# Rwkv scan on one core: second BETA times V and first inverse in turn ahead of level 2, keys of both chunks in turn

## The reference, cut to what matters

```python
def wkv7_scan(s0, r, w, kk, a, k, v):
    def step(s, inp):
        r_t, w_t, kk_t, a_t, k_t, v_t = inp
        s_kk = jnp.einsum('bhvk,bhk->bhv', s, kk_t)
        s = (s * w_t[:, :, None, :] - s_kk[..., None] * (kk_t * a_t)[:, :, None, :]
             + v_t[..., None] * k_t[:, :, None, :])
        return s, jnp.einsum('bhvk,bhk->bhv', s, r_t)
```

## Time and profile before

| | |
|---|---|
| median of 3 runs | 3761.28 us (3754.23 to 3763.72) |
| profiled execution | 3748.89 us |
| its span | 3747.1 us |
| mean granted TensorE clock | 0.904 of full |
| TensorE matmul busy | 3128.4 us (83%) |
| VectorE busy | 1132.6 us (30%) |
| the scan in the trace | from about 447 to 992 us |

### The profile page before, as it was taken

One profiled execution on the slowest core, in us unless ns is written; L12 is line 12 of the kernel. 1 busy time (PEld: TensorE's weight loads), 2 busy tenths in 40 slices (PEclk: granted clock), 3 DMA queues, 4 the chain that ended last, 5 costly groups with the idle time before them and its releaser, 6 DMA issues. The chain is left out here.

```text
span 3747.1 us, 61863 instructions
## 1 busy us (share of the span) xinstructions
PE 3128.4 (83%) x27303; PEld 2140.8 (57%) x27303; DVE 1132.6 (30%) x1902; ACT 544.8 (15%) x995; POOL 198.7 (5%) x170
## 2 busy tenths in 40 slices
PE   3998489999887999985999999875977488877874
PEld 1454378888533444442999999862436254544442
DVE  0302477777442111345111111014013562110112
ACT  0001233333201000011000010101011141100001
POOL 0000012111100000000100000000001000100000
PEclk8999689999979999987999999987985698899997
DMA  8322312211405324604677777723100104899995
GB/s 348 125 70 78 93 50 56 69 51 27 152 3 124 97 79 153 250 35 153 200 271 279 245 256 279 251 76 113 68 1 0 62 1 180 335 427 426 427 427 201
DMA packets 246708, 612.13 MB, mean 163 GB/s; under 512 B 27188, under 2 KB 136278, under 8 KB 230968
## 3 DMA queue, kind: packets, MB, share of 16 engines
q1 hardware_dynamic: 217704, 522.93, 37.9%
q10 hardware_dynamic: 15968, 54.41, 3.8%
q0 software_dynamic: 12784, 30.99, 3.0%
HBM read 565.64 MB, written 42.63 MB: 162 GB/s over the span
## 5 line engine op out<-in xcount | busy, mean ns | idle before, releaser
L2655 PE MATMUL ps<-moe_xt,moe_wb 128*128 128x152 f32 (+1 forms) x3520 | 457.2, 292 | 2.5 <-DVE moe_xt L2817 1.9
L2655 PEld LDWEIGHTS ps<-moe_xt,moe_wb 128*128 128x128 f32 x3520 | 452.5, 194 | 3.1 <-issue 3.1
L1614 PE MATMUL ps<-ffn_h,ffn_wb 128*128 128x512 f32 x704 | 304.2, 595 | 15.5 <-PEq L1509 15.5
L2333 PE MATMUL ps<-hier_wb,hier_xt 128*64 128x256 f32 x2048 | 241.1, 391 | 73.7 <-DMA hier_wb<-in_expert_w_up 38.1
L2333 PEld LDWEIGHTS ps<-hier_wb,hier_xt 128*64 128x64 f32 x2048 | 160.0, 141 | 166.2 <-issue 66.2
L1614 PEld LDWEIGHTS ps<-ffn_h,ffn_wb 128*128 128x128 f32 x704 | 134.4, 191 | 185.3 <-issue 185.3
L2662 PE MATMUL ps<-moe_hT,moe_wb 128*128 128x152 f32 (+1 forms) x1760 | 227.2, 290 | 0.0
L2662 PEld LDWEIGHTS ps<-moe_hT,moe_wb 128*128 128x128 f32 x1760 | 222.7, 190 | 0.0
L834 PE MATMUL ps<-AT,X 64*64 64x64 f32 x4608 | 162.5, 225 | 33.2 <-DVE X L1120 18.1
L834 PEld LDWEIGHTS ps<-AT,X 64*64 64x64 f32 x4608 | 152.1, 139 | 44.9 <-issue 24.3
L1683 PE MATMUL ps<-ffn_g,ffn_wd 128*128 128x512 f32 x352 | 153.0, 598 | 2.6 <-PEq L1577 2.6
(11 more groups left out here) (487 smaller groups left out, 4063.8 us busy)
## 6 DMA issues: line engine op xcount, KB each, us to landing
moe_wb<-in_moe_w SPq DMA_DIRECT2D x60, 2048.0 KB, 10.4
hier_wb<-in_expert_w_gate SPq DMA_DIRECT2D x32, 2048.0 KB, 38.1
hier_wb<-in_expert_w_up SPq DMA_DIRECT2D x32, 2048.0 KB, 38.1
hier_wb<-in_expert_w_down SPq DMA_DIRECT2D x32, 2048.0 KB, 38.4
moe_wb<-in_moe_w SPq DMA_DIRECT2D x30, 1536.0 KB, 7.7
wb_ada<-in_ada_w SPq DMA_DIRECT2D x8, 3072.0 KB, 18.5
ada_late<-in_ada_w ACTq DMA_DIRECT2D x8, 3072.0 KB, 9.6
ffn_wb<-in_ffn_w SPq DMA_DIRECT2D x22, 1024.0 KB, 7.8
```

The lines of the kernel that those rows point to most:

```text
L1614: mm = pe.matmul(k.ps[:, bank + q, :], wb[:, j, q, c, o * P:(o + 1) * P], h[:, c, :], start=c == 0, stop=c == KC - 1)
L2333: mm = pe.matmul(k.ps[both_halves(a), bank, 0:256], xs[:, c, :], wb[:, slot, at:at + 256], start=c == 0, stop=c == KC - 1)
L2655: mm = pe.matmul(k.ps[:, bank, 0:width], wb[:, slot, at:at + P], xs[:, c, :], start=c == 0, stop=c == KC - 1)
```

## The change

In `b_times_v` and `inverse_times` the single products become functions (`one_b_times_v`, `one_inverse_times`) with the same operands and places in PSUM. The first chunk's BT times V and the second chunk's inverse keep their places. The first chunk's inverse leaves its place behind level 2: it is issued ahead of level 2, right behind `prep_sums`, where the second chunk's BT times V already stood, and product by product in turn with that. Both now stand behind the waits of both. The keys of both chunks are issued head by head in turn. The number of products is unchanged.

```diff
+                def inverse_and_second_b_times_v(n):
+                    need(pe, w_taken, 2 * n + 1)
+                    need(pe, updated, 2 * NL * (n + 1))
+                    need(pe, bt_sb, min(n + 2, TILES))
+                    need(pe, gt_sb, outputs(min(n + 1, TILES - 1)))
+                    for h in range(2 * HP):
+                        b = one_b_times_v(n, 1, h)
+                        t_w = one_inverse_times(n, 0, h)
+                        if h == 2 * HP - 1:
+                            b.then_inc(bv_ps, 1)
+                    t_w.then_inc(u_ps, 1)
...
-                def keys_to_state(n, step):
-                    if step == steps(n):
-                        return
-                    r = rows_of(chunk_of(n, step))
+                def keys_to_state(n):
...
                     for h in range(2 * HP):
-                        cols = slice(h * C, (h + 1) * C)
-                        pe.matmul(k.ps[half(h), 4 + step, hcols(h)], tok_k[r, n % 2, cols], V[r, n % 3, cols],
-                                  start=h < 2, stop=False)
+                        for step in range(steps(n)):
+                            r, cols = rows_of(chunk_of(n, step)), slice(h * C, (h + 1) * C)
+                            pe.matmul(k.ps[half(h), 4 + step, hcols(h)], tok_k[r, n % 2, cols], V[r, n % 3, cols],
+                                      start=h < 2, stop=False)
...
                     if nxt:
                         prep_sums(n + 1)
                     if prev:
-                        b_times_v(n - 1, 1)
+                        inverse_and_second_b_times_v(n - 1)
                     if now:
                         level_change(n, 2)
                     if prev:
-                        inverse_times(n - 1, 0)
-                        keys_to_state(n - 1, 0)
-                        keys_to_state(n - 1, 1)
+                        keys_to_state(n - 1)
                         betas_to_state(n - 1, 0)
```

More of the change, by code:

```diff
@@ L865, in prep_sums, with one_b_times_v @@
                     mm.then_inc(sums_ps, 1)
[L867 to L876, removed]
+                def one_b_times_v(n, step, h):
+                    r = rows_of(chunk_of(n, step))
+                    return pe.matmul(k.ps[r, 2 + h % 2, hcols(h)], BT[r, n % 2, slot(h), :],
+                                     V[r, n % 3, h * C:(h + 1) * C], start=h < 2, stop=False)
@@ new lines, in one_inverse_times, with first_b_times_v @@
+                def one_inverse_times(n, step, h):
+                    r = rows_of(chunk_of(n, step))
+                    return pe.matmul(k.ps[r, 2 + h // 8, h % 8 * C:h % 8 * C + C], TT[r, slot(h), :],
+                                     wb[r, h * C:(h + 1) * C], start=True, stop=True)
+                def first_b_times_v(n):
+                    need(pe, bt_sb, n + 1)
+                    need(pe, v_landed[n % 3], 16 * (n // 3 + 1))
+                    need(pe, u_taken, 2 * n)
+                    need(pe, gt_sb, outputs(n))
@@ L877, in b_times_v @@
                     for h in range(2 * HP):
-                        mm = pe.matmul(k.ps[r, 2 + h % 2, hcols(h)], BT[r, n % 2, slot(h), :],
-                                       V[r, n % 3, h * C:(h + 1) * C], start=h < 2, stop=False)
+                        mm = one_b_times_v(n, 0, h)
                     mm.then_inc(bv_ps, 1)
+                def inverse_and_second_b_times_v(n):
[9 more added lines that the diff above has]
+                    t_w.then_inc(u_ps, 1)
@@ L882, in kappa_times_state, with second_inverse_times @@
+                def second_inverse_times(n):
+                    need(pe, w_taken, 2 * n + 2)
+                    for h in range(2 * HP):
+                        mm = one_inverse_times(n, 1, h)
+                    mm.then_inc(u_ps, 1)
                 def kappa_times_state(n, step):
@@ L890, in kappa_times_state @@
                     mm.then_inc(w_ps, 1)
-                def inverse_times(n, step):
-                    r = rows_of(chunk_of(n, step))
[L894 to L902, removed]
-                def keys_to_state(n, step):
-                    if step == steps(n):
-                        return
-                    r = rows_of(chunk_of(n, step))
+                def keys_to_state(n):
                     if n + 2 < TILES:
@@ L999, in _ @@
                             output_from_state(n - 1)
-                        inverse_times(n - 1, 1)
+                        second_inverse_times(n - 1)
                     if now:
@@ L1005, in _ @@
                     if now:
-                        b_times_v(n, 0)
+                        first_b_times_v(n)
                         last_turn(n)
```

## The result

The changed kernel takes 3733.81 us in the median of 5 runs (3727.72 to 3738.91), against 3754.23 us for the kernel before on the same chip (3749.52 to 3763.72). The ratio is 0.9941 with a 95% interval of 0.9920 to 0.9961: 22 us faster, at the least 15. The forecast was 9 us faster, and the range ended at 3740. The wait that the forecast counted is gone, but the gain is twice its size.

What follows compares the result with a forecast made beforehand. A tile was a VectorE stretch, then a TensorE stretch, joined by the wait at L1161. Gains of 3.1, 4.4, 1.1 and 0.5 us summed to 9.1, from the median 3761.28 to 3752.2 us; range 3740 to 3766.

Steps and rivals of the forecast that it cites:

- The wait that the forecast counted: VectorE's wait at L1161 for the betas of step 0, ahead of the new state: 0.68 us in iteration 8, 13.4 in all.
- The pair takes 1.93 us in place of 3.55: First inverse and b_times_v in turn ahead of level 2 run at a level's pace, saving TensorE 1.62 us a tile.
- The rival that the two would not run in turn: Shared PSUM banks hold the pair to 3.6 us, level 2 comes late, ten tiles lose 0.6 us each: 3767; chance 0.05.
- The keys at the pace of four quarters: Keys of both chunks in turn take output_from_tile's 1.07 us in place of 1.69, saving 0.62.
- They are worth nothing beside the pair: Even without any gain on the keys, the betas' sum comes 0.9 us before VectorE needs it.
- u is taken behind the exponentials, VectorE's wait goes, TensorE waits some 1.3 us for level 3's masks: At the joint: u there 2.6 us earlier, VectorE's 0.68 us wait gone, a new TensorE wait ahead of level 3.
- 9.1 us from the wait: Over the scan: 3.1 us from context iterations, 4.4 from latent ones, 1.1 from iteration 11, 0.5 from the last.
- The last iteration: 0.5 us: The pair waits until 973.15 for TT's update and ends at 975.1 in place of 975.7.
- What is lost at the tile's end: Rival: TensorE's stop in level 5, up to 4.32 us, swallows the latent 4.4 us (3756.6) or all (3761); chance 0.15.
- the clock falls; this is the case on the other side: Rival: the new wait ahead of level 3 lowers the clock, 1.8 us each, 20 us in eleven iterations: 3772; chance 0.1.
- TensorE's saving arrives whole: Rival: VectorE's stretch is not the limit, so TensorE's saved work counts in full, some 26 us: 3735; chance 0.1.

Runs made afterwards that it cites:

- the pair alone: Against the kernel before, only the first inverse and b_times_v in turn ahead of level 2, keys one chunk after the other as before: 3734.53 us, ratio 0.9948.
- small loads: Both kernels, with r, k and kk loaded on 8 of 128 partitions from the second tile on: 3805.30 us (kernel before) and 3795.65 us (changed).
- late loads: Both kernels, with hw and ha loaded first and r, k and kk held until BT is kept: 3734.72 us (kernel before) and 3714.52 us (changed).
- the keys alone: Kernel before with only the keys of both chunks in turn, everything else as before: 3750.15 us, ratio 0.9986.
- the inverse moved but not paired: As the changed kernel, keys in turn included, but b_times_v first and then the first inverse, not in turn: 3753.73 us, ratio 0.9997 to the kernel before.
- the betas late: Changed kernel with the betas of step 0 issued behind level 3 in place of ahead of it: 3786.29 us, ratio 1.0087.

## Why the prediction was wrong

Point by point:

- *The pair takes 1.93 us in place of 3.55.* Right: 1.9 to 2.0. The rival that the two would not run in turn is out: they share banks 2 and 3 at this pace. The Trainium skill ("TensorEngine Tiling (Array Packing)", Gotcha 1) has it that row tiles cannot use one PSUM bank at a time; the measurement differs, and decides: the pair and the levels both run at 30 ns an instruction, where half of the pair's products and all of a level's meet in one bank. The two write different partitions of the bank here.
- *The keys at the pace of four quarters.* Right in kind: 0.94 us, even below the 1.07 taken. *They are worth nothing beside the pair*: right, by the pair alone.
- *u is taken behind the exponentials, VectorE's wait goes, TensorE waits some 1.3 us for level 3's masks.* Right: 806.61 behind 805.87 + 0.65, no wait, 1.34 us.
- *9.1 us from the wait.* Right: 8.9 by the waits, and the tiles at full clock agree.
- *The last iteration: 0.5 us.* Right: its wait went from 5.0 to 4.5.
- *What is lost at the tile's end.* Nothing was: TensorE's stops sum to 23.9 to 25.1 us in the scans before and 24.1 to 24.3 us after.

**The step that failed** is the sum, from the wait to the whole. It takes the clock as it was, and has a term for it on the slow side alone ("the clock falls; this is the case on the other side"). The prediction itself shows a fall of the kernel before, in a context tile; that such falls could become fewer was put at nothing, without a reason. The scan is 15.7 us shorter in the mean of three profiles each. 8.9 are the wait. The time at half clock went from 29.1 to 16.5 us in the mean, 12.6 less. One microsecond of it costs TensorE half a microsecond of its work. What it costs a tile is from 0.2 us (the two latent tiles above) to 0.6 us (the context tile of iteration 2 in the kernel before took 40.5 us with some 3 at half clock, and 38.5 without, with no stop in either). By half it would be 6.3 us and the scan would be accounted for; by the cheaper latent tiles it is less, and a few microseconds stay without an owner. The stops give almost nothing. The same arithmetic fits the other pairs: small loads, 8.7 of wait and half of 12.4, 14.9 against 13.6; late loads, 8.5 less half of 3.6, 6.7 against 6.7. So the wait's mechanism was right, and the missing term has up to two thirds of its size.

Why there is less time at half clock stays open. Over the scan it is less in each of three profiles of the changed kernel than in any of three before, and the kernels with the pair alone (18.0) and without the pair in turn (24.8, 26.6) lie on their sides. But tile by tile the kernels overlap: iterations 6 to 10, where the stops are, have about 14, 24 and 7 us in the three profiles before and 0, 14 and 10 after. Much of the rest of the difference is in iterations 2 to 5, with about 3, 0 and 10 us before and none in the three after. What each fall hangs on isn't shown.

The second failure is smaller: the prediction had no term outside the scan. The spans differ by 21.4 us in the mean of the three; the first mark comes 1.8 us later after the change, the scan gives 15.7, and 7.5 lie behind it. 4.4 of these are the gap between the last product of the first mixture and the second block's first norm, where no code was changed (84 to 91 us before, 83 after). It opens with a wait for rows that are fetched (`moe_yg`), and most of the difference is there: until VectorE has the first of them it takes 29 to 31 us where the gap is 82 to 84, and 35 to 36 where it is 87 to 91. The gap was also about 91 with the keys alone and with the late loads of the kernel before, 84 with the inverse moved but not paired, 82 with the pair alone and with the late loads of the changed kernel, and 83 with the betas late. With small loads, where other data come in, it was 80 and 89, the other way round. So it isn't simply the change, and chance can't be told from build here: its cause was not tried and stays open.

The 3 us that are left go with the clock again. Behind the scan the kernel before has 568, 592 and 576 us at half clock, the changed one 548, 569 and 559. That is 20 less in the mean, some 14 of them outside the gap. Over the twelve profiles with all data loaded, what follows the scan is by and large the longer the more of it is at half clock: from 2746 us with 552 at half clock to 2762 us with 582 and with 592. They go together; no run changed the clock there alone.

This can be checked on more than three profiles, since the runs without a trace give their mean granted clock too. It is 0.9023 in 66 runs of the kernel before and 0.9043 in 12 of the changed one: 734 and 715 us at half clock over the whole kernel, at mean times of 3754.5 and 3734.8. Among the 66 runs of the one kernel, a line through time against half clock rises by 0.36 us for each microsecond, and among the 12 by 0.21. An estimate from these: of the 19.7 us the clock has 4 to 7, the wait 8.9, and some 4 to 7 have no owner. So the clock is a real part of the gain, but three profiles each made it look larger than it is (31 us less at half clock over the whole kernel, in place of 19).

The range should have reached below 3740: the rival "TensorE's saving arrives whole" at 3735 had been given one chance in ten, and the range stopped 5 us short of it; the prediction calls that half way, but it is 12 of the 17 us from the forecast. The time came near that number, by another way.

## What to carry to other kernels

A wait at the joint of two engines was worth what its row says, and a pace read from neighbouring groups of the same kind held; but where the granted clock already falls in some stretches, give the change a term for it with both signs, take several profiles before calling the clock's share noise or gain, and look at the granted clock of all runs. Look at what is loaded while an engine stands still for nothing that the profile names: moving three loads by a few microseconds gave 20 us here, as much as the whole change. And matmuls of one quarter of the array belong between matmuls of another: 30 in place of 56 ns each here.

## What the runs showed that I had not expected

- TensorE's unnamed stops hang on the inputs' load. With full loads at the tile's end they are 2 to 4.3 us; with small or late loads mostly 0.6 to 1.4 us.
- The pace by quarters, from weight load to weight load, is 56 ns for one quarter, 30 for two, 15 for four (0.94 us for 64 keys), and 26 ns where the rows stay and the columns alternate.
- A wait inserted at the joint cost twice what it was worked out at: 2.5 us in each tile at full clock, 28 us in all, came with 52 us of time and 85 us at half clock.
